# Gated embedding kept in PSUM: where sigmoid, product, residual sum and low parts are made, and how their statistic is summed

## What is computed

```
x = x + (silu(gate) * (h @ w_up[i])) @ w_down[i]
ple_gate = jax.nn.sigmoid(rmsnorm(x, g_ple[i]) @ w_ple_gate[i])
x = x + ple_gate * (p[i].astype(x.dtype) @ w_ple_proj[i])
...
hn = rms_norm(x, norm_mix_pre[l])
mix = hybrid_mixer(hn, w_in[l], ...)
```

## Time and profile before

| | us |
|---|---|
| median of 3 runs (1329.9 to 1331.58) | 1330.01 |
| the profiled execution's own time | 1330.1 |
| its span in the trace | 1328.0 |
| TensorE matmul busy | 1285.4 (97%) |
| VectorE busy | 684.0 (52%) |
| ScalarE busy | 379.1 (29%) |
| GpSimd busy | 770.2 (58%) |

### The profile page before, as it was taken

How to read it: one execution, slowest core, us unless ns; L and a number is a source line. 1 busy time by engine, 2 the same in 40 slices (tenths; PEclk the granted TensorE clock), 3 DMA queues, 4 the chain that set the end, 5 groups by cost and what they waited for, 6 DMA issues and landing times. The chain is left out here.

```text
span 1328.0 us, 16141 instructions
## 1 busy us (share of the span) xinstructions
PE 1285.4 (97%) x6436; PEld 1055.5 (79%) x6436; DVE 684.0 (52%) x918; ACT 379.1 (29%) x674; POOL 770.2 (58%) x472
## 2 busy tenths in 40 slices
PE   7999989999999999999999999999899999999996
PEld 5788878878888888888877778778788888888885
DVE  6453654677445442113785968685578544440002
ACT  4322354222111211003226456473332211111000
POOL 6854523587666647668665445224749766656662
PEclk9999989999999999999989999999899999999998
DMA  7222211323333323233332122102132333323331
GB/s 279 80 64 80 79 33 48 96 94 96 96 98 99 103 69 114 91 97 125 95 95 82 63 80 65 49 17 68 60 111 95 96 95 96 96 74 96 97 97 64
DMA packets 35502, 117.32 MB, mean 88 GB/s; under 512 B 3956, under 2 KB 4468, under 8 KB 35300
## 3 DMA queue, kind: packets, MB, share of 16 engines
q1 hardware_dynamic: 34272, 114.13, 27.2%
q10 hardware_dynamic: 1156, 2.16, 0.5%
HBM read 114.18 MB, written 2.10 MB: 88 GB/s over the span
## 5 line engine op out<-in xcount | busy, mean ns | idle before, releaser
L411 POOL TENSOR_TENSOR WL<-RAW,WH 128x1024 fp32r<-128x1024 f32 (+2 forms) x226 | 516.0, 2283 | 18.9
L408 POOL TENSOR_SCALAR WH<-RAW 128x1024 fp32r<-128x1024 f32 (+2 forms) x226 | 236.6, 1047 | 469.1 <-DMA RAW<-in_w 439.4
L454 PE MATMUL PS<-AH,WH 128*128 128x512 f32 x896 | 351.8, 393 | 9.1 <-DVE AL L1612 9.1
L456 PE MATMUL PS<-AH,WL 128*128 128x512 f32 x896 | 349.4, 390 | 0.0
L455 PE MATMUL PS<-AL,WH 128*128 128x512 f32 x896 | 349.4, 390 | 0.0
L454 PEld LDWEIGHTS PS<-AH,WH 128*128 128x128 f32 x896 | 168.5, 188 | 47.6 <-issue 10.0
L456 PEld LDWEIGHTS PS<-AH,WL 128*128 128x128 f32 x896 | 168.6, 188 | 35.3
L455 PEld LDWEIGHTS PS<-AL,WH 128*128 128x128 f32 x896 | 168.7, 188 | 34.8 <-issue 0.2
L456 PE MATMUL PS<-SH,WL 128*128 128x512 f32 x352 | 136.9, 389 | 0.0
L454 PE MATMUL PS<-SH,WH 128*128 128x512 f32 x352 | 136.9, 389 | 0.0
L455 PE MATMUL PS<-SL,WH 128*128 128x512 f32 x352 | 136.9, 389 | 0.0
(11 more groups left out here) (352 smaller groups left out, 1833.9 us busy)
## 6 DMA issues: line engine op xcount, KB each, us to landing
RAW<-in_w SPq DMA_DIRECT2D x163, 512.0 KB, 3.5
RAW<-in_w SPq DMA_DIRECT2D x32, 384.0 KB, 3.0
RAW<-in_w SPq DMA_DIRECT2D x32, 320.0 KB, 2.9
X<-in_x SPq DMA_DIRECT2D x4, 512.0 KB, 6.6
BT<-in_bias SPq DMA_DIRECT2D x1, 2048.0 KB, 8.0
out<-X SPq DMA_DIRECT2D x4, 256.0 KB, 2.5
out<-X ACTq DMA_DIRECT2D x4, 256.0 KB, 2.7
PIN<-in_p ACTq DMA_DIRECT2D x1, 512.0 KB, 4.3
```

What stands on the lines that cost most here:

```text
L408: nc.gpsimd.tensor_scalar(WH[:, slot, 0:width], RAW[:, slot, 0:width], 1.0, 1.0, ALU.mult, ALU.mult).then_inc(s_hi, 1)
L411: nc.gpsimd.tensor_tensor(WL[:, slot, 0:width], RAW[:, slot, 0:width], WH[:, slot, 0:width].bitcast(F32), ALU.subtract).then_inc(s_split, 1)
L454: nc.tensor.matmul(o, lh, rh, start=start, stop=False)
L456: return nc.tensor.matmul(o, ll, rh, start=False, stop=stop)
```

## The change

Sigmoid writes into PSUM banks 4, 5, 2, 3 in turn (SBANK) in place of SG, which is gone. VectorE multiplies there with PP, and adds X there too, the sum staying in the bank. ScalarE then copies the sum back into X (an added activation for each tile) and makes GH and the square as before. VectorE makes GL from the bank, not from X. Since banks 4 and 5 are used by tiles 4 and 5 last, TensorE waits for the low part of tile 5 (the sixth) before the first `bva` unit; and from tile 4 on the sigmoid waits for the low part of the tile four before it, which frees its bank. The last square isn't added to ACC: the statistic becomes two parts, ACC and the last SQ, each with its 128x512 matmul and its four one-column matmuls, summed in PSUM. The square of tile 6 is added behind the loop. `stages` counts one addition less for "mix2".

```diff
-        SG = put("SG", [P, DK, T], F32, S_at + 32 * KB)
...
+        SBANK = (4, 5, 2, 3)
...
+            def statistic_in_parts(n, bank):
+
+                for part, src in enumerate((ACC, SQ[:, 1, :])):
+                    if part:
+                        ge(pe, s_sq[n], DK)
+                    else:
+                        ge(pe, s_acc[n], DK - 1)
+                    nc.tensor.matmul(pb[bank], INVD, src[:, 0:T], start=(part == 0), stop=(part == 1))
                     for t in range(NT):
-                        ins = nc.tensor.matmul(pb[bank + 1][:, t:t + 1], ACC[:, tokens(t)], INVD[:, 0:1],
-                                               start=True, stop=True)
+                        ins = nc.tensor.matmul(pb[bank + 1][:, t:t + 1], src[:, tokens(t)], INVD[:, 0:1],
+                                               start=(part == 0 and t == 0), stop=(part == 1 and t == NT - 1),
+                                               skip_group_check=True)
                 ins.then_inc(s_ms[n].sem, 1)
...
             ge(pe, s_sd["ple"], 1)
+            ge(pe, s_gl["mix2"], 6)
             for n in range(2):
                 value_unit("bva", n, n, s_gl["mix2"])
...
-            statistic("mix2", True, bank=2)
+            statistic_in_parts("mix2", 2)
...
                     act.wait_ge(s_pgt, m + 1)
-                    A(SG[:, m, :], TMP[:, m % 2, :], ACT.Sigmoid).then_inc(s_sg, 1)
+                    if m >= 4:
+                        ge(act, s_gl["mix2"], m - 3)
+                    A(pb[SBANK[m % 4]], TMP[:, m % 2, :], ACT.Sigmoid).then_inc(s_sg, 1)
                 if m >= 2:
+                    act.wait_ge(s_pm, 2 * (m - 1))
+                    A(X[:, m - 2, :], pb[SBANK[(m - 2) % 4]], ACT.Copy).then_inc(s_x["mix2"].sem, 1)
                     norm_tile("mix2", "pre2", (m - 2) // 2, 2, m % 2, GH)
...
-            def g4(m):
-                low("mix2", "pre2", m // 2, 2, m % 2, GH, GL)
-                add_square("mix2", m // 2, 2, m % 2)
+            def gl_low(m):
+                ge(dve, s_gh["mix2"], m + 1)
+                V_.scalar_tensor_tensor(GL[:, m, :], pb[SBANK[m % 4]], prm("pre2", m), GH[:, m, :].bitcast(F32),
+                                        ALU.mult, ALU.subtract).then_inc(s_gl["mix2"].sem, 1)
...
-                    V_.tensor_tensor(SG[:, n, :], SG[:, n, :], PP[:, n, :], ALU.mult).then_inc(s_pm, 1)
-                    dve.wait_ge(s_pm, n + 1)
-                    V_.tensor_tensor(X[:, n, :], X[:, n, :], SG[:, n, :], ALU.add).then_inc(s_x["mix2"].sem, 1)
+                    V_.tensor_tensor(pb[SBANK[n % 4]], pb[SBANK[n % 4]], PP[:, n, :], ALU.mult).then_inc(s_pm, 1)
+                    dve.wait_ge(s_pm, 2 * n + 1)
+                    V_.tensor_tensor(pb[SBANK[n % 4]], pb[SBANK[n % 4]], X[:, n, :], ALU.add).then_inc(s_pm, 1)
                 if m >= 2:
-                    g4(m - 2)
+                    gl_low(m - 2)
+                if 2 <= m < DK:
+                    add_square("mix2", (m - 2) // 2, 2, m % 2)
+            add_square("mix2", 3, 2, 0)
```

More of the change, by code:

```diff
@@ L298, in build @@
         s_gh, s_gl = stages("gh", SPLIT, DK), stages("gl", SPLIT, DK)
-        s_sq, s_acc = stages("sq", ALL, DK), stages("acc", ALL, DK, LAST)
+        s_sq, s_acc = stages("sq", ALL, DK), stages("acc", ALL, DK, LAST + ("mix2",))
         s_diag, s_bcast = stages("diag", LAST, 2), stages("bcast", LAST, 1)
@@ L511, in row_unit, with statistic @@
                 return ins
-            def statistic(n, with_columns=False, bank=6):
+            def statistic(n):
                 ge(pe, s_acc[n], DK)
-                ins = nc.tensor.matmul(pb[bank], INVD, ACC[:], start=True, stop=True)
-                if with_columns:
+                nc.tensor.matmul(pb[6], INVD, ACC[:], start=True, stop=True).then_inc(s_ms[n].sem, 1)
+            def statistic_in_parts(n, bank):
[5 more added lines that the diff above has]
+                    nc.tensor.matmul(pb[bank], INVD, src[:, 0:T], start=(part == 0), stop=(part == 1))
                     for t in range(NT):
-                        ins = nc.tensor.matmul(pb[bank + 1][:, t:t + 1], ACC[:, tokens(t)], INVD[:, 0:1],
-                                               start=True, stop=True)
+                        ins = nc.tensor.matmul(pb[bank + 1][:, t:t + 1], src[:, tokens(t)], INVD[:, 0:1],
+                                               start=(part == 0 and t == 0), stop=(part == 1 and t == NT - 1),
+                                               skip_group_check=True)
                 ins.then_inc(s_ms[n].sem, 1)
```

## The result

The changed kernel takes **1334.85 us** (median of 16 runs, 1333.13 to 1338.1), the kernel before 1329.95 (16 runs beside it, 1325.61 to 1338.03): ratio 1.0037, with an interval of 1.0022 to 1.0052, so slower by 2.9 to 6.9 us. The forecast was 1331.2 within 1329.2 to 1333.3; the time lies above it. The profiled execution took 1334.94 us, 4.8 more than that of before, and its mean granted clock is 0.986.

What follows compares the result with a forecast made beforehand. TensorE, busy 97%, was taken as the bound. Removed 7.9 us against 3.7 + 3.6 + 0.1 = 7.4 put in gives minus 0.5; plus 1.7 for the clock, plus 1.2: 1331.2 us, range 1329.2 to 1333.3.

Steps and rivals of the forecast that it cites:

- The serial chain before `bva`: Before the first `bva` unit, TensorE waits through scaling, sigmoid, copy, high and low part: 3.6 us, 3.7 with slow first matmul.
- The PSUM operands: In the gate rounds, 24 VectorE operations lose one SBUF operand and take 0.69 us each, the low part 0.74.
- The scaling of unit 7 at once: At the last gate unit, VectorE scales right after the matmul, at 669.66, 3.7 us earlier than before.
- The statistic: After `small`, two 128x512 matmuls and two sets of columns take 3.6 us at full clock, against 3.30 at half.
- `k0` at the full rate: Behind the statistic, with no stop before it, `k0` runs at full clock: 1.62 us less, lasting 5.5 to 5.8.
- The clock behind the stop: After the new stop before `bva`, the granted clock falls to half: 1.7 us lost, between nothing and 3.4.
- removed 7.9 us: From first `bva` to decay gates, waits and half clock go: 1.05 at `small`, 1.96 and 3.30 at the statistic, 1.62 at `k0`.
- a lone stop of 2.49 us does not fall: Near 795 us, a lone TensorE stop of 2.49 us between dense matmuls left the clock at 1.00.
- No fall: Rival: the clock stays full at the new stop before `bva`, time 1329.5 us; chance 0.20.
- A second fall at the statistic: Rival: one-column matmuls of the two-part statistic make the clock fall again, 1332.9 us, or 1336.3; chance 0.16.
- No protection: Rival: PSUM operands don't protect VectorE, unit 7 is scaled at 673.35, TensorE stands 3.7 us longer, 1334.9 us; chance 0.06.
- Faster: Rival: the wait before `bva` is already met when TensorE arrives, so stop and fall go, 1325.8 us; chance 0.03.

Runs made afterwards that it cites:

- e8: The changed kernel once more, unedited, for a third trace of one profiled execution: 1334.68 us.
- e12: The changed kernel again, unedited, timed beside other kernels: 1332.83 us, ratio 1.0019 to the kernel before.
- e16: The kernel before, unedited, timed as a kernel of its own with a fourth trace: 1328.49 us, ratio 0.9995.
- e5: The kernel before, unedited, one profiled execution for a second trace: 1327.74 us.
- e6: The kernel before, unedited, one profiled execution for a third trace: 1324.93 us.
- e1: Changed kernel with sums in banks 6, 7, 2, 3 and TensorE waiting only before the third and fourth row of `bva`: 1327.79 us, ratio 0.9988 to before.
- e11: Changed kernel with banks 6, 7, 2, 3 and waits per row, one-part statistic, and root-column operations behind the eviction of `small`: 1327.01 us, ratio 0.9982 to before.
- e3: The kernel before with one added line, TensorE waiting for the sixth low part before the first `bva` unit: 1338.24 us, ratio 1.0071 to before.
- e13: Changed kernel with the statistic in one part, all eight squares added, timed a second time: 1334.64 us, ratio 1.0046 to before.
- e14: Changed kernel with one-part statistic and the root columns' reciprocal and halving moved behind the eviction the gates wait for: 1331.6 us, ratio 1.0013 to before.
- e2: Changed kernel with the statistic in one part, all eight squares added, first timing: 1337.25 us, ratio 1.0064 to before.
- e4: Changed kernel with banks 6, 7, 2, 3 and waits per row, plus the statistic in one part: 1326.73 us, ratio 0.9987 to before.

## Why the prediction was wrong

**What was right.** The serial chain before `bva`: forecast 3.6 to 3.7 us, measured 3.52 of stop and 3.67 in the start of `bva`. The PSUM operands: forecast 0.69, and 0.74 for the low part; measured 0.69, 0.70 and 0.75. That also answers the cycle table which the prediction quoted from the page "VectorE: DVE Perf Modes" of the Trainium skill: the fixed 65 ns more for a PSUM operand don't show (the additions with two SBUF operands in the same loop take 0.68). The scaling of unit 7 at once: forecast 669.66 for a matmul that ends at 669.63, measured 671.90 for one that ends at 671.87. The statistic: 3.6 forecast, 3.42 measured. `k0` at the full rate: 5.66. The clock behind the stop: forecast 1.7; the five traces give 1.7, 1.7, 1.7, 2.6 and 0.1, 1.6 in the mean. That size is partly luck: the forecast put it together from 6.8 us at half clock with a part inside the stop, and in three traces it was 3.4 us, all behind the restart; only e8 had the 6.8 with a part inside, and lost 2.6. What the change puts into the stretch was thus forecast at 7.4 + 1.7 = 9.1 us and measured, as a mean of five traces, at 30.89 - 22.33 = 8.6 (22.33 is the prediction's 21.8 + 0.3, and 0.23 for the last gate matmul). The warning of the page "TensorE: Matmul & The Clock Gate" of the Trainium skill that the prediction cited holds in four traces of five, and not in e12. It speaks of long idle gaps only, longer than the stops at 689, 795 and 949, so it was read too widely where those rows were said to agree or not.

**The step that failed** is the first term of the sum, "removed 7.9 us", together with the sentence that the sum is made against the profiled execution's own time and the median lies 0.1 below it. In the profile before the 7.9 us were there, and in e16 as well. In e5 and e6 only 24.38 - 22.33 = 2.05 and 2.11 us were there to be removed. The mean over the four traces is 27.34 - 22.33 = 5.0. With that in the sum: 9.1 - 5.0 = plus 4.1 instead of plus 1.2; with the measured 8.6 it is plus 3.6. The change removes a loss that two of the four traces don't have, and puts in a stop that all five have. How often the loss comes in untraced executions is not known, so the 5.0 is a mean of four and no more.

The profile had a sign of it: the stop hung on one addition with two SBUF operands, and the earlier trace rows has such operations of 128x512 at 0.74, 2.22 and 2.88 us, by what GpSimd did beside them. The prediction used this very thing to explain why VectorE was late, and gave the removed stops no range. A low end could have been worked out from the same rows: without the 1.05, the 1.96, half of the statistic's 3.30 and the 1.62 of `k0`, some 1.6 us would remain of the 7.9, and the upper end of the range would lie about 6 us higher.

**The rest.** Of 4.9 us between the medians (2.9 to 6.9), the stretch holds 3.6 in the mean of five and four traces. Every kernel with the changed code, e1 and e11 too, takes a further 0.3 us between the first level products and 795 us. In the timeline of TensorE a stop is there that before doesn't have:

```profile
748.20 0.49 PE L890 MATMUL PS<-LVS 64*128 64x128 f32 x4 [0.39 <-ACT SAB L1447]
```

It goes back to ScalarE, whose four evictions AO stand ahead of that one. In after and then in before:

```profile
744.81 2.42 ACT L1464 ACTIVATE AO<-PS,COL 128x512 f32<-128x512 f32 x4 [1.96 <-issue]
```

```profile
741.48 2.42 ACT L1451 ACTIVATE AO<-PS,COL 128x512 f32<-128x512 f32 x4 [1.67 <-issue]
```

In all 13 traces with changed code they begin 0.30 to 0.33 us behind the first level product, after 1.96 to 1.98 us of idle time; in the five with the code of before (e3 too) 0.03 to 0.04 behind it, after 1.67 to 1.69. What ScalarE does in that time the traces don't name, so the cause is open. Then, at the stop of 2.5 us near 795 the clock fell in four of five traces of after and in one of four of before, about 1.55 us each time, 0.9 in the mean. With so few traces that may be chance, and it is not shown that the change has to do with it: of the eight other traces with changed code five had the fall and three hadn't, and e3, with the code of before, had it. It does show the second weak inference: "a lone stop of 2.49 us does not fall" was one execution's course too. The mean spans differ by 5.3 us (1331.8 and 1326.5); the 0.5 that is left beside 3.6, 0.3 and 0.9 lies before the stretch, whose start varies by 2 us among the traces of either kernel (669.24 to 671.39 in before, 669.56 to 671.64 in after).

**The rivals.** "No fall" occurred in one trace of five. "A second fall at the statistic" in none. "No protection" is refuted by the groups above, and e3 shows what it would have cost, 5.3; that its 1334.9 is the time measured is a coincidence of numbers. "Faster" was said to be excluded by the order on ScalarE; that holds for banks 4 and 5, but e1 shows that with another choice of banks, and the wait set per row, TensorE doesn't stand for it. The case that came about stood among none of them: that the kernel before often isn't as slow there as in its profile.

## What to carry to other kernels

Where a stop hangs on one operation that is sometimes three or four times as long, look at two or three executions before a gain is booked for its removal, or take the unstretched duration as the low end. Work that is moved into PSUM should take the banks that the next matmuls write last: this change costs 0.4% with banks 4 and 5 (0.2% in e12), and with 6 and 7 it can't be told from before. Small operations belong behind the eviction for which TensorE waits, not ahead of it: 3.0 us between e13 and e14.

## What the runs showed of the hardware

- The same stop of 3.52 us in the same code was followed by 3.4 us at half clock in three traces, 6.8 in one and none in one; in e13 and e14, which have the same stop, by 3.4, and in e2 by 6.8. Where it was 3.4 us it began 0.7 to 1.3 us behind the restart; where it was 6.8 it began inside the stop. A stop of 2.11 was followed by 3.4 us of half clock, and one of 0.76 by none. The stop of 2.5 us near 795 went both ways with the code of before and with the changed code.
- A wait of only 0.61 to 0.65 us before the gates' narrow matmuls (32 rows) was followed by 3.4 us of half clock in e2, e3 and e13 and cost 1.6 us; in e4, with 0.68, it wasn't (the part from the gates to the levels took 41.96 us; 41.98 in after). Why e4 differs is open.
- Contention with GpSimd stretches a VectorE operation on 128x4 elements, too: 1.14 and 1.16 us in e13 and e2 while GpSimd splits weights, 0.17 in after behind it. That is the halving (TENSOR_SCALAR); the reciprocal of the same 128x4 just ahead of it took 0.17 to 0.18 us in every trace, beside GpSimd's low part as well (697.45 in e13). The part of the Trainium skill cited at e16 speaks of operations with two SBUF inputs or in a mode that takes both ports; the halving has one input, and which mode it runs in no run here shows.
- VectorE with one operand in PSUM was not held up beside GpSimd in any of the 17 products, sums and low parts of after that ran beside a low part of weights (of all 24, 689 ns the shortest, 751 the longest; the addition with two SBUF operands of e16 took 2.84 us).
